# A hybrid decoder trunk on eight cores: the first norm, LayerNorm and the attention block chains emitted in order of estimated readiness, and copies spread over the conv loop

## What is computed

```python
def run(x, p, conv_past, kv_past):            # once for the prompts, once for the samples
    h = x
    # layer 0
    hn = rms_norm(h, norm_mix[0])
    a, gate = split(hn @ w_pw1 + b_pw1)       # 1024 -> 2048
    u = a * sigmoid(gate)
    c = depthwise_conv31(concat([past, u])) + b_dw      # causal, per channel
    c = silu(layer_norm(c, ln_g, ln_b))
    h = h + c @ w_pw2 + b_pw2
    h = h + swiglu(rms_norm(h, norm_ffn[0]), w_gate, w_up, w_down)          # 2816 wide
    h = h + sigmoid(rms_norm(h, norm_ple[0]) @ ple_gate) * (p[0] @ ple_proj)
    k, v = shared_kv(h)                       # 4 heads of 64, k normed
    # layer 1
    q = project_q(rms_norm(h, norm_mix[1]))   # 16 heads, normed
    h = h + sink_attend(q, k, v, window 128, sinks) @ w_o   # samples: 128 cached keys + 1
    h = h + moe(rms_norm(h, norm_ffn[1]))     # top 2 of 8 experts, 3584 wide
    h = h + sigmoid(rms_norm(h, norm_ple[1]) @ ple_gate) * (p[1] @ ple_proj)
```

## Time and profile before

| | us |
|---|---|
| median of three runs | 3597.19 |
| lowest and highest of them | 3272.71, 3692.99 |
| the profiled execution | 3274.39 |
| its span (first to last instruction, slowest core, core 1) | 3273.3 |
| span of the fastest core (core 7) | 3230.8 |
| mean granted PE clock, core 1 | 0.922 |

### The profile page before, as it was taken

One profiled execution on the slowest core, in us unless ns is written; L12 is line 12 of the kernel. 1 busy time (PEld: TensorE's weight loads), 2 busy tenths in 40 slices (PEclk: granted clock), 3 DMA queues, 4 the chain that ended last, 5 costly groups with the idle time before them and its releaser, 6 DMA issues.

```text
span 3273.3 us, 50984 instructions; the slowest of 8 cores (3230.8 to 3273.3 us)
## 1 busy us (share of the span) xinstructions
PE 2839.6 (87%) x18083; PEld 1617.0 (49%) x18083; DVE 1169.4 (36%) x2115; ACT 831.1 (25%) x1498; POOL 369.1 (11%) x575
## 2 busy tenths in 40 slices
PE   4589679999987777686699999999999999999957
PEld 2333235555533443343476566566666666666523
DVE  3122554666655566456121111111111111111058
ACT  4132441111114555444221111111111111111034
POOL 2000010000002232313000000000000000000032
PEclk8799899999988788777799999999999999999979
DMA  6954313999321010303389766777776677776567
GB/s 174 171 121 99 90 56 63 297 289 256 83 50 38 19 43 24 69 17 102 88 142 163 137 129 127 140 146 145 139 136 129 129 141 140 148 137 135 118 208 240
DMA packets 135267, 415.44 MB, mean 127 GB/s; under 512 B 14763, under 2 KB 44267, under 8 KB 118403
## 3 DMA queue, kind: packets, MB, share of 16 engines
q0 software_dynamic: 44176, 238.13, 39.6%
q1 hardware_dynamic: 89971, 167.71, 16.9%
q10 hardware_dynamic: 864, 6.25, 1.1%
...
...
## 4 chain that ended last, share of the span: by engine, by line
PE 76%; DVE 7%; DMA 7%; issue 4%; ACT 3%; POOL 1%; SPq 0%; DVEq 0%; ACTq 0%; POOLq 0%; another core or an unknown queue 0%
PE pb L264 67%; PE pb L320 3%; DVE arena L313 2%; DMA arena<-xg_rows 2%; PE pb L516 2%; PE pb L666 1%; ACT arena L307 1%; DMA arena<-b_pw 1%; PE pb L1627 1%; DMA arena<-y_rows,arena 1%; PE pb L1035 1%; DMA arena<-u_rows 1%; DMA arena<-moe_gu 1%; DMA arena<-consts 1%; POOL arena L310 0%
## 5 line engine op out<-in xcount | busy, mean ns | idle before, releaser
L264 PE MATMUL pb<-arena 128*128 128x320 bf16 (+4 forms) x13728 | 2355.9, 333 | 21.2 <-ACT arena L1204 5.7
L264 PEld LDWEIGHTS pb<-arena 128*128 128x128 bf16 x13728 | 1332.0, 99 | 1015.3 <-issue 124.1
L1490 DVE TENSOR_TENSOR arena<-arena,pb 128x320 bf16<-128x320 f32 x448 | 218.4, 488 | 1040.3 <-PE pb L264 1016.9
L1489 ACT ACTIVATE arena<-pb 128x320 f32<-128x320 f32 x448 | 195.8, 437 | 911.8 <-PE pb L264 910.0
L320 PE MATMUL pb<-arena 128*128 128x128 bf16 (+1 forms) x1536 | 155.0, 264 | 257.2 <-DVE arena L313 173.4
L320 PEld LDWEIGHTS pb<-arena 128*128 128x128 bf16 (+1 forms) x1536 | 124.1, 120 | 296.3 <-issue 290.2
L770 DVE TENSOR_TENSOR arena<-arena,pb 128x512 f32<-128x512 f32 (+1 forms) x374 | 244.2, 682 | 38.3 <-PE pb L264 25.1
L126 POOL DMA_DIRECT2D arena<-moe_gu x112 | 59.3, 530 | 1336.5 <-PE pb L264 1090.4
L313 DVE SCALAR_TENSOR_TENSOR arena<-arena 128x1024 bf16<-128x1024 f32 (+1 forms) x119 | 149.4, 1279 | 56.4 <-POOL arena L310 51.5
L758 ACT ACTIVATE arena<-pb 128x413 f32<-128x413 f32 (+1 forms) x110 | 56.7, 516 | 398.2 <-DVE arena L770 215.0
L307 ACT ACTIVATE arena<-arena 128x1024 bf16<-128x1024 f32 (+1 forms) x102 | 107.4, 1054 | 94.6 <-DVE arena L926 30.8
...
## 6 DMA issues: line engine op xcount, KB each, us to landing
arena<-moe_gu POOLq DMA_DIRECT2D x112, 1024.0 KB, 9.4
...
arena<-u_rows SPq DMA_DIRECT2D x96, 135.0 KB, 3.2
...
```

Of the source, the lines that this page charges most:

```text
L264: last = e.matmul(banks[bk][0:prow, 0:ncols], l, rr, start=(i == 0), stop=(i == len(pairs) - 1))
L1489: S.op("act", lambda e: e.activation(out=sil[k][:, 0:HALF], in_=banks[bA][:, 0:HALF], func=AF.Silu), r=[b_r_[bA]], w=[sil_r[k]])
L1490: S.op("dve", lambda e: e.tensor_tensor(out=hact[e_ % 2][:, fi, cs], in0=sil[k][:, 0:HALF], in1=banks[bB][:, 0:HALF], op=ALU.mult), r=[sil ...
```

## The change

All engines' instructions of the three stages are now emitted in the order of a clock that the program keeps as it is built. `Sched.order` gives every instruction a start (its engine free, its inputs written 0.1 before, its output buffer read) and an end from a length `d` written beside it (2.5 for eight Silus, 0.00043 a column for matmuls; 3.0 until a DMA lands). `flow(gens, depth)` keeps up to `depth` generators alive and always advances the one whose last instruction ends first by that clock.

- Front: norms and the five products go through one `flow` of depth 7; `load_w1(1)` is issued by the third product.
- `late_loads`, `params`, W2, the three DRAM copies (now on SP's queue), b_pw2, gF0 and the four `history` steps are called from `spread(c)` at the end of conv loop iteration c; `past` has one buffer, loaded four times.
- cb is laid out by blocks; `LN(t)` works by block and `ln_out` emits eight Silus of 128 columns as one step; LN and PW2 share a `flow` of depth 9.
- Chains: `yield "name"` marks the border of a part that one block holds at a time (a1, a1b, a2, a2b, a2c, b1, b2, b2b, r); nearly every instruction is its own step; the transpose of the attention's output moves from B1 to B2; xaT, xkT, xqT and ob get a second buffer, qTb has two instead of three, kTb three instead of four; B1 emits the scores of a group two ahead. The masks are 128 columns wide and broadcast over four heads. The last down product is one more generator of the same `flow`, depth 10.

The diff, cut to its core:

```diff
+    def order(self, e, d, lat, r, w, after):
+        t = self.vt[e]
+        for x in r:
+            t = max(t, x.tw + 0.1)
+        for x in list(w) + list(after):
+            t = max(t, x.tw + 0.1, x.tr + 0.1)
+        self.vt[e] = t + d
+        end = t + d + lat
+        for x in r:
+            x.tr = max(x.tr, end)
+        for x in w:
+            x.tw = end
+        self.nem += 1
+        if lat == 0:
+            self.tmax = max(self.tmax, end)
...
+    def flow(gens, depth):
+        live = []
+        while gens or live:
+            while gens and len(live) < depth:
+                live.append([gens.pop(0), 0.0, False])
+            free_ = [x for x in live if not x[2]]
+            if not free_:
+                for x in live:
+                    x[2] = False
+                free_ = live
+                stuck[0] += 1
+                assert stuck[0] < 1000
+            x = min(free_, key=lambda y: y[1])
+            n0 = S.nem
+            S.tmax = 0.0
+            done = True
+            for _ in x[0]:
+                done = False
+                break
+            if S.nem > n0:
+                stuck[0] = 0
+                x[1] = S.tmax + 0.05
+                for y in live:
+                    y[2] = False
+            elif not done:
+                x[2] = True
+            if done:
+                live.remove(x)
+                for y in live:
+                    y[2] = False
+
+    stuck = [0]
...
+    cb = [view(t * 16384, [128, 32, 128]).rearrange("p (b c) q -> p b c q", b=4) for t in range(4)] + [view(65536, [128, 8, NS])]
...
+    def load_past(g4):
+        S.dma("sp", past, sc[g4 * 4:g4 * 4 + 4, :, :].rearrange("a j d -> (a j) d"), "past", w=[past_r], after=xb0_r[0:2])
...
+        while b >= 4 and b - 4 not in done0:
+            yield
...
+    def pw1f(t):
+        while not set(range(4 * t, min(4 * t + 4, 17))) <= done0 or (t > 0 and ("p", t - 1) not in done0):
+            yield
+        if t == 2:
+            load_w1(1)
+        yield from pw1s(0, t)
+        done0.add(("p", t))
+        if 1 <= t < 4:
+            stack(0, t - 1)
...
+    flow([norm0(b) for b in range(4)] + [pw1f(0)] + [norm0(b) for b in range(4, 8)] + [pw1f(1)] + [norm0(b) for b in range(8, 12)] + [pw1f(2)]
+         + [norm0(b) for b in range(12, 17)] + [pw1f(3), pw1f(4)], 7)
...
-    S.dma("act", ks[:, 0:127, :], ck[:, 1:128, :], "d2d")
-    S.dma("act", vs[:, 0:127, :], cv[:, 1:128, :], "d2d")
-    S.dma("act", convs[:, 0:29, :], sc[:, 1:30, :], "d2d")
-    wl(W2.rearrange("p k f -> p (k f)"), w2p, "w2", W2_r, after=xst_r[3:6] + xb0_r[2:4])
-    S.dma("pool", b2hl[0:1, :], b_pw2[:, :], "b2", w=[b2_r])
-    gload(gF0, norm_ffn[0:1, :], "gF0", gF0_r)
...
+    def spread(c):
+        if c == 0:
+            late_loads()
+        if c == 1:
+            params()
+        if c == 2:
+            wl(W2.rearrange("p k f -> p (k f)"), w2p, "w2", W2_r, after=xst_r[3:6] + xb0_r[2:4])
+            S.dma("pool", b2hl[0:1, :], b_pw2[:, :], "b2", w=[b2_r])
+        if c == 3:
+            S.dma("sp", ks[:, 0:127, :], ck[:, 1:128, :], "d2d")
+        if c == 4:
+            S.dma("sp", vs[:, 0:127, :], cv[:, 1:128, :], "d2d")
+            for h_ in range(2):
+                hs = slice(h_ * 512, h_ * 512 + 512)
+                S.dma("sp", b2f, b_pw2[:, hs], "b2f", w=[b2lo_r])
+                S.op("pool", lambda e: e.tensor_tensor(out=b2t[:, hs], in0=b2f, in1=b2hl[0:1, hs], op=ALU.subtract), r=[b2_r], w=[b2lo_r])
+            S.dma("sp", b2hl[1:2, :], b2t, "b2l", r=[b2lo_r], w=[b2_r])
+        if c == 5:
+            S.dma("sp", convs[:, 0:29, :], sc[:, 1:30, :], "d2d")
+            gload(gF0, norm_ffn[0:1, :], "gF0", gF0_r)
+        if 1 <= c < 5:
+            history(c - 1)
...
+    def ln_out(b, src, r):
+        c0, nr = CT[b]
+
+        def fs(e):
+            last = None
+            for c in range(8):
+                last = e.activation(out=sT[:, c, c0:c0 + nr], in_=src[:, c, :], func=AF.Silu, bias=pcol(LNB + c), scale=pcol(LNG + c))
+            return last
+        S.op("act", fs, r=r + [par_r], w=[sTb_r[b]], after=[xnT_r[b]], d=2.5)
+        ln_done.add(b)
...
-        for q4 in range(4):
-            cs = slice(q4 * 2, q4 * 2 + 2)
-            S.op("dve", lambda e: e.tensor_tensor(out=C[:, cs], in0=C[:, cs], in1=banks[bR][:, :].unsqueeze(1).to_broadcast([128, 2, 512]), op=ALU.mult),
-                 r=[b_r_[bR]], w=C_r[cs])
-            S.op("dve", lambda e: e.tensor_tensor(out=C[:, cs], in0=C[:, cs], in1=banks[bN][:, :].unsqueeze(1).to_broadcast([128, 2, 512]), op=ALU.add),
-                 r=[b_r_[bN]], w=C_r[cs])
-            if q4 == 3:
-                rl(bR, bN)
-            ln_out(t, range(q4 * 2, q4 * 2 + 2))
-            yield
-        ln_x(t)
+        S.op("pe", lambda e: e.matmul(banks[bR][:, :], selbc[:, t, :], lnR, start=True, stop=True), r=[selbc_r, tmp_r[0]], w=[b_r_[bR]], d=0.9)
+        S.op("pe", lambda e: e.matmul(banks[bN][:, :], selbc[:, t, :], lnN, start=True, stop=True), r=[selbc_r, tmp_r[1]], w=[b_r_[bN]], d=0.9)
+        yield
+        for bi in range(4):
+            b = 4 * t + bi
+            C = cb[t][:, bi, :, :]
+            qs = slice(bi * 128, bi * 128 + 128)
+            S.op("dve", lambda e: e.tensor_tensor(out=C, in0=C, in1=banks[bR][:, qs].unsqueeze(1).to_broadcast([128, 8, 128]), op=ALU.mult),
+                 r=[b_r_[bR]] + cb_r[t], w=[cbB_r[b]], d=1.2)
+            S.op("dve", lambda e: e.tensor_tensor(out=C, in0=C, in1=banks[bN][:, qs].unsqueeze(1).to_broadcast([128, 8, 128]), op=ALU.add),
+                 r=[b_r_[bN]], w=[cbB_r[b]], d=1.2)
+            yield
+            ln_out(b, C, [cbB_r[b]])
+            ln_x(b)
+            yield
+        rl(bR, bN)
...
+        while b not in ln_done:
+            yield
...
-        if c == 0:
-            params()
+        spread(c)
...
-    tick(LN(0))
-    while live:
-        tick()
-    ln_out(4, range(8))
-    ln_x(4)
+    ln_out(16, cb[4], cb_r[4])
+    ln_x(16)
+    todo = []
     for t in range(4):
-        if t < 3:
-            live.append(LN(t + 1))
-        drive([PW2(b) for b in range(4 * t, 4 * t + 4)] + ([PW2(16)] if t == 0 else []), 2, 1)
-    while live:
-        tick()
+        todo += [LN(t)] + [PW2(b) for b in range(4 * t, 4 * t + 4)] + ([PW2(16)] if t == 0 else [])
+    flow(todo, 9)
...
+    xaT_.append(cn([128, 8, 128], BF16))
...
+    qTb = [T3([128, 8, 128], BF16) for _ in range(2)]
+    kTb = [T3([128, 2, 128], BF16) for _ in range(2)] + [view(205632, [128, 2, 128], BF16)]
...
-        bKV, bQ0, bQ1 = yield from get(3)
-        bQ = (bQ0, bQ1)
+        yield "a2b"
+        bKV, = yield from get(1)
+        bQ = []
...
+        def sc_m(g):
+            for kb, pi in zip(kbs, pidx(g)):
+                S.op("dve", lambda e: e.tensor_tensor(out=Pt[pi].rearrange("p (j q) -> p j q", j=4), in0=Pt[pi].rearrange("p (j q) -> p j q", j=4),
+                                                      in1=(maskc if kb == b else maskp).unsqueeze(1).to_broadcast([128, 4, 128]), op=ALU.mult), r=[par_r], w=[P_r[pi]], d=0.45)
+            yield
...
+        yield from sc_p(0)
+        yield from sc_e(0)
+        yield from sc_p(1)
+        yield from sc_m(0)
+        yield from sc_e(1)
         for g in range(4):
+            yield from pv(g)
+            if g + 2 < 4:
+                yield from sc_p(g + 2)
             if g + 1 < 4:
-                yield from scores(g + 1)
-                yield
-            yield from pv(g)
-            yield
-        yield
-        bk, = yield from get(1)
-        tr8(bk, ob, 128, [ob_r])
-        S.op("act", lambda e: e.copy(out=oT, in_=tr8_out(bk, 128)), r=[b_r_[bk]], w=[oT_r])
-        rl(bk)
-        yield
+                yield from sc_m(g + 1)
+            if g + 2 < 4:
+                yield from sc_e(g + 2)
...
+    def locked(g):
+        cur = None
         for v in g:
-            if v == "next":
-                held.discard(name)
-                name += "+"
-                while name in held:
+            if v is None:
+                yield
+            else:
+                while v in held:
                     yield
-                held.add(name)
-            else:
-                yield
-        held.discard(name)
+                held.add(v)
+                held.discard(cur)
+                cur = v
+        held.discard(cur)
...
+    def last_down():
+        for b, h_ in DL:
+            fdn(NFB - 1, b, h_)
+            if h_ == 1:
+                done_fd.add(b)
+            yield
+        for en in ("act", "dve", "pool", "sp"):
+            S.deps(en, [], [gu_r3[1], dn_r3[1]])
+        wl(Wo.rearrange("p k f -> p (k f)"), wop, "wo", Wo_r, after=xnF_r + [r_ for l_ in hF_r[0] for r_ in l_])
+        done_fd.add(99)
...
     def chain(b):
-        yield from seg("A1", A1(b))
-        yield from seg("A2", A2(b))
-        yield from seg("B1", B1(b) if b < 16 else B1s())
-        yield from seg("B2", B2(b))
-        if b == GRP[G_OF[b]][-1]:
```

(47 more changed lines are left out.)

461 lines of the change are left out of this document (262 added, 199 removed).

## The result

| | before | after |
|---|---|---|
| median on one chip, four runs each, us | 3439.28 | 3328.24 |
| lowest | 3272.71 | 3180.97 |
| the profiled execution | 3274.39 | 3183.96 |
| its span, core 1 | 3273.3 | 3182.9 |
| span of core 7 | 3230.8 | 3146.6 |

The ratio after / before is 0.972, 95% interval 0.968 to 0.976: the change saves 2.8%, some 90 us, where 149 were forecast. Both kernels have executions that are some per cent longer at a lower clock on one die; they are in the medians (so 3328 lies above the predicted range of 3050 to 3205, which was made for an execution like the profiled one), the ratios leave them out, and the experiments' stages are read from cores that ran undisturbed in that stage.

The account below looks back on a forecast made before the run. Bound taken: TensorE (PE) idle or at low clock in front, LayerNorm part and block chains; SwiGLU and experts have nothing to give. 3274 - 37 - 27 - 86 = 3124, forecast 3125 us, range 3050 to 3205.

Parts of the forecast that it names:

- LayerNorm: LayerNorm with second pointwise product: block-by-block work emitted by readiness takes 112 us, saving 27; bounds -40 and -5.
- beats: Block chains: time between router copies falls from 31.2 to 27.3 us a block, saving 62 us over 16.
- the saving at the chains' start: Block chains' start: first router copy comes 100 us after the SwiGLU instead of 124, saving 24 us.
- (a): Front: moving cache and state copies and the W2 load from before the conv loop removes PE's whole idle time, -22 us.
- (c): Front: norms and five products ordered by readiness, late loads moved behind them; stretch of 84.7 us becomes 70, -15.
- (b): Front: four history steps move into the conv loop; -19 us before it, +14 inside at 3.5 each, net -5.
- rival 3: Conv loop: copies hold SP's queue, PE stands 12 us three times; +31 us on the +5, total 3156; chance 0.08.
- 85% use of the fullest: LayerNorm and second product: fullest of three engines with 82 to 86 us each is 85% used, giving 101 us.
- at 86% use: Block chains: PE's 23.5 us of work a block at clock 0.91, with PE 86% used, gives 27.3 us.
- Rival 2: Chains: beat hardly moves, 30.5 us, as serial part b1's steps queue behind other work; 61 us more, 3186; chance 0.20.
- Rival 1: Chains: an engine becomes the bound, PE close to full at high clock; beat 24.3, 48 us less, 3077; chance 0.20.
- rival 4: Chains: waiting parts keep PSUM banks from b1, beat lengthens to 39 us; slower than before, 3311; chance 0.04.

Follow-up runs that it names:

- Part b1 preferred: The changed kernel with the block holding part b1 advanced as if ready 4 us earlier; the beats took 480 to 490 us instead of 443 to 453.

## Where the prediction was right and where it failed

The forecast execution was 3125, the measured one 3184: inside the predicted range, at 60% of the forecast gain. By its own terms, on core 1: front -14.5 for -37, LayerNorm -7.5 for -27, beats -48.4 for -62, start -1.2 for -24, end +0.9 for 0; and 19 us less in the experts, for which there was no term. The misses add up to 79 us, less those 19. The sum's step that failed first is the saving at the chains' start; the other terms have the right sign and are short in size. (The best case that the prediction left out of its range is added up wrongly: its own bounds give -55 for the front and -139 for the chains, so 3040, not 3037 from -47 and -150. The forecast doesn't rest on it.)

**Front: (a) right, (c) right, (b) mis-sized, and one thing not foreseen.** The stall went whole (-24.4 with the copies alone for -22). Norms, late loads and history together gave -33.5 before the loop for -34. The copies in SP's queue and the b_pw2 loads behind them cost at most 3 us (219.6 without history against 216.7) for +5. By the Trainium skill (DMA: Bandwidth & Descriptors, section on queues, rings and completion order) a row's ring is worked in order, which is rival 3. The copies and the stack loads do share SP's row here, and no wait of PE for a stack load in the loop of after is over 1.7 us; whether the loads stood behind the copies in the rings, no run here shows. The history steps came back at 20.7 us instead of 14. "PE needs 1.92 us at the full clock" was the wrong one of the two rows: the four took 13.3 us, 3.3 each, which is 5.6 of the 6.7 us missing. The wait (1.4 each for 1.59) was right, and slower work behind the steps, not counted, is about 2. Moving them gained nothing: 19 us before the loop, by the prediction's estimate, against 20.7 in it. On core 7 the front's sum is -34.3 for -37. On core 1 some 20 us more went, for which the next section has the reason.

**LayerNorm: mis-sized in two terms.** Eight Silus of 128 columns take 3.2 us, 0.40 each for 0.36, so ScalarE has 87 us of work for 82; PE has 97 us (core 1) to 104 (core 7) for 86, since its clock was taken as full and is 0.90 and 0.85. With these, "85% use of the fullest" and 11 us on top give 133 us on core 7 and 126 on core 1; measured to the first product of the SwiGLU were 130.4 and 129.3. So the sizes put in were off, and the share of use was near. Two long Silus a block give 119 to 125, so half to two thirds of what was missing hangs on the cut into 128 columns that the new order brought along, though ScalarE was not the fullest engine.

**Chains, start: the step that failed is "saved at the start".** It took 100 us from an own chain of 80, and 123.0 was measured for 124.2. The last down product, which part B1 of block 0 waits for, is mixed in by readiness and ends 58 us after the SwiGLU instead of 44, and the `pp` wait stayed. But even with both mended only 1 to 7 us came, and with six chains alive the start is 3 to 8 us shorter. What holds the rest stays open. PE did more in the same time (95.5 us of work for 82.4 on core 7, 538 matmuls for 425), on blocks behind the first. That work is missing from the beats, which have 116 matmuls fewer: part of what was forecast for the start came there.

**Chains, beat: right in sign, short in size.** 28.1 us for 27.3; without the work done early in the start it would have been longer, so the nearness is in part luck. The failed link is "at 86% use": PE is used 74% of the stretch, as before (73.5%), with the clock at 0.81 for 0.91. In the beats the clock was higher where PE was busier: 0.77 at 74% in before, 0.85 at 79% without masks, 0.88 at 87% with the masks on PE; but after itself has 0.81 at the 74% of before. Of PE's 107 idle microseconds on core 7, 81 stand in the waits shown under "Part b1 preferred" and one of 5.7 for the router: the masks of b1 (27), the key cache (18, which the prediction named and gave no term), the attention's output on its way to the transposes (15.4 + 6.5 = 22), and a norm (8). Rival 2 had the place right: taking one VectorE step out of b1's serial chain gives 22 to 38 us. Its queueing half is not borne out, since preferring b1 makes it worse. Why cores 0 to 3 gained less than 4 to 7 from the masks on PE stays open; the runs show only that PE waits there 16 to 24 us for the attention's output, and 13.8 on each of the others.

Rival 1 needed a full engine and there is none (PE 74%, VectorE 59%, ScalarE 49%). Rival 3 fell with the copies alone and the kernel without history steps, rival 4 with the result itself and the depth of six.
